# Experts of a mixture in blocks of 32 rows on four column groups of TensorE, with plain float32 weights

## The chip, the core and the metric

The kernel runs on one core of a Trainium2 chip. The metric is the time of one execution on the device in microseconds (us). An execution is also profiled; its trace gives the start, the duration and the releaser of each instruction and the packets of each DMA.

## What is computed

A trunk of two layers runs over 1280 tokens of width 1024 (256 of context, 1024 latent). Layer 0 mixes tokens by a convolution, layer 1 by gated linear attention, and each is followed by a hierarchical mixture of 32 experts: the best of 4 groups, then the best two of its 8 experts. Layer 0 routes 1280 tokens (2560 pairs of token and expert), layer 1 only the 1024 latent ones (2048 pairs). The expert itself is:

```python
def block_ffn(args):
    e, idx = args
    xb = h_pad[idx]
    return (jax.nn.silu(xb @ w1[e]) * (xb @ w3[e])) @ w2[e]
```

`w1[e]` and `w3[e]` are 1024 x 512, `w2[e]` is 512 x 1024, all float32: 6.29 MB an expert, 201 MB a layer. The sum over a token's two experts, weighted by the router, goes back into the residual. Everything is float32.

## The kernel before

Every phase is a function that writes one program for each engine, with semaphores between them and a barrier at its end: `front`, `conv_taps`, `conv_out`, then `route`, `experts` and `combine_values` for layer 0, then `gla_keys`, `gla_scan`, `gla_output`, and `route`, `experts`, `combine` for layer 1.

`route` sorts the pairs by expert into blocks of `BLK` = 128 rows, so that no block holds rows of two experts, and writes a plan: the token of each row, the expert of each block, and whether a block begins a new expert (`fresh`). The experts are taken in a fixed order, the first of each group, then the second of each, and so on.

`experts` runs over the blocks, whose number is known only at run time. For a block GpSimd gathers 128 token rows (L1335), TensorE turns them (`turn_x`, L1367), ScalarE and VectorE split the result into a high part in the short type fp32r and a low part, and the product with each weight is made of three fp32r matmuls of 512 columns (`product3`, L100 to L102). The weights are split in the same way, once an expert: ScalarE writes `moe_w_hi` (L1426), VectorE writes `moe_w_lo` (L1497). SyncE loads them ahead (L1295), each half of a matrix by a DMA of 1 MB: two buffers for `w1` and `w3`, one for `w2`; a load waits until VectorE has split what the buffer held. ScalarE takes the finished block out of PSUM (L1436) and stores it, a row of 1024 values to a row of `yd` (L1440). In the layer 0 pass SyncE also writes zeros into the blocks of `yd` that stay unused (L1320). `combine_values` and `combine` gather from `yd`.

`front` has the only matmuls of the kernel before that stand in column groups: `acc[j * STRIP:j * STRIP + 2, 0:P]` (L230), four outputs of 2 rows that begin at rows 0, 32, 64 and 96 of PSUM. It also loads tables of few rows from ScalarE's queue: `dw_w` has 31 rows, `pw1_b` 2, `norm_g` 8, and four tables one.

Of the kernel before, what the change touches and what calls it, by code (L numbers as in the profile page):

```python
# [27 lines left out]
GROUPS, PER_GROUP, EXPERTS, FF, BLK = 4, 8, 32, 512, 128  # L28
# [323 lines left out]
def conv_taps(nc, d, ht, vt, vecs, cs, mod, raw, ada_w, w2_raw):  # L352
# [3 lines left out]
    with ExitStack() as ctx:  # L356
# [12 lines left out]
        ahead = ph.sb("ahead", [P, CONV_W // 2 - 1])  # L369
        acc = [ph.sb(f"acc{q}", [P, HALF_OUT]) for q in range(2)]  # L370
# [21 lines left out]
        with nc.Block() as block:  # L392
# [39 lines left out]
            def _(pool):  # L432
                pool.memset(one[:, :], 1.0).then_inc(s("one_set"), 1)
                for b in range(2):
                    pool.memset(u[b][:, :, :], 0.0).then_inc(s("u_zero"), 1)
                for at in range(total):
# [49 lines left out]
            def _(act):  # L486
# [21 lines left out]
                for n in range(KC):  # L508
                    for g, (t0, m, c0) in enumerate(CONV_GROUPS):
# [13 lines left out]
                act.wait_ge(s("w2_hi"), KC)  # L523

# [462 lines left out]
def route(nc, d, layer, streams, plan, lg, ranks):  # L987

# [7 lines left out]
    with ExitStack() as ctx:  # L996
        ph = Phase(nc, ctx, f"route{layer}")
        s = ph.sem
        next_e = ph.sb("next_e", [P, EXPERTS])
        before = ph.sb("before", [P, P])  # L1000
        ones = ph.sb("ones", [P, P])
        ident = ph.sb("ident", [P, P])
        iota = ph.sb("iota", [P, P])
        token = ph.sb("token", [P, TILES])
        gm = ph.sb("gm", [P, nt])
        ga = ph.sb("ga", [P, nt, GROUPS])
        gsel = ph.sb("gsel", [P, nt, GROUPS])
        gw = ph.sb("gw", [P, nt])
        inner = [ph.sb(f"inner{j}", [P, nt, EXPERTS]) for j in range(2)]
        cand = ph.sb("cand", [P, nt, EXPERTS])  # L1010
        least = ph.sb("least", [P, nt])
        top = ph.sb("top", [P, 2, nt])
        hot = ph.sb("hot", [P, 2, nt, EXPERTS])
        both = ph.sb("both", [P, nt, EXPERTS])
        sofar = ph.sb("sofar", [P, nt + 1, EXPERTS])
        rank = ph.sb("rank", [P, nt, EXPERTS])
        picked = ph.sb("picked", [P, 2, nt, EXPERTS])
        mine = ph.sb("mine", [P, 2, nt])
        first = ph.sb("first", [P, 2, nt])
        over = ph.sb("over", [P, 2, nt])  # L1020
        steps = ph.sb("steps", [P, nt])
        more = ph.sb("more", [P, 2 * nt * nt + EXPERTS * nt])
        need = ph.sb("need", [P, EXPERTS])
        ends = [ph.sb(f"ends{j}", [P, EXPERTS]) for j in range(2)]
        passed = ph.sb("passed", [P, EXPERTS])
        blk_col = ph.sb("blk_col", [P, 1])
        blk = ph.sb("blk", [1, nb + 2])
        fresh = ph.sb("fresh", [1, nb])
        in_slot = ph.sb("in_slot", [P, 2 * nt, P])
        in_blk = ph.sb("in_blk", [P, 2 * nt, nb + 1])  # L1030
        pr = ph.ps("pr", [P, nt * EXPERTS])
        pa = ph.ps("pa", [P, nt * EXPERTS])
        pi = ph.ps("pi", [P, nb + 1])
        pb = ph.ps("pb", [1, P])

        with nc.Block() as block:
            @block.sync
            def _(sp):
                for dst, src in ((iota[:, :], d.iota), (before[:, :], d.before), (ones[:, :], d.ones), (token[:, :], d.token),
                                 (next_e[:, :], d.next_expert[0].partition_broadcast(P)), (ident[:, :], d.ident)):  # L1040
                    sp.dma_start(dst, src).then_inc(s("loaded"), 16)

            @block.tensor
            def _(pe):
                pe.wait_ge(s("loaded"), 96)
                pe.wait_ge(s("chosen"), 1)
                pe.matmul(pr[:, :], before[:, :], both[:, :, :].rearrange("p t e -> p (t e)"), start=True, stop=True)
# [21 lines left out]
            def _(dve):  # L1069
# [70 lines left out]
                for j in range(2):  # L1140
                    link(dve.tensor_tensor(picked[:, j, :, :], hot[:, j, :, :], rank[:, :, :], ALU.mult))
# [1997 lines left out]
```

## Time before, and how its profile is read

| what | us |
|---|---|
| median of 3 runs (lowest, highest) | 3011.33 (3010.84, 3011.63) |
| the profiled execution, and the span of its trace | 3014.36, 3012.5 |
| layer 0: route, from start to the start of experts | 688.9 to 726.5 |
| layer 0: experts, to the start of combine | 726.5 to 1526.0 |
| layer 1: route | 2277.2 to 2308.9 |
| layer 1: experts, to the start of combine | 2308.9 to 2933.0 |

PE is TensorE, PEld its loads of the stationary operand, DVE VectorE, ACT ScalarE, POOL GpSimd, SP SyncE; a queue of the DMA engines is named q0 (issued by GpSimd), q1 (by SyncE) or q10 (by ScalarE). A busy time is read against the stage in which it stands, and a mean over the span hides stages with different limits. Matmuls overlap, so their rate is read from the starts of groups. A plain float32 matmul leaves two records in the trace.

### The profile page before, as it was taken

The numbers are of one execution on the slowest core, as the hardware profiler recorded it, in microseconds if no ns is written. First come the engines' busy times: TensorE is split into PE (matmuls) and PEld (weight loads), VectorE is DVE, ScalarE is ACT, GpSimd is POOL, SyncE is SP. The second block draws the span as 40 slices with busy tenths as digits, with TensorE's granted clock in tenths as the row PEclk, the third lists the DMA queues.
The fourth block names the chain that finished last, engine by engine and source line by source line (L and its number), as shares of the span: only waits on it lengthen the run. The fifth ranks groups of instructions, "written<-read, shape, count | busy, mean of one in ns | idle before, by whom it ended". The sixth has DMA issues, their size and how long they took to land. (4 is left out here: it accounts for less than half of the span.)

```text
span 3012.5 us, 41138 instructions
## 1 busy us (share of the span) xinstructions
PE 2510.7 (83%) x13498; PEld 2036.1 (68%) x13498; DVE 1993.3 (66%) x2023; ACT 1449.3 (48%) x1624; POOL 346.5 (12%) x400
## 2 busy tenths in 40 slices
PE   6788761993999999999929989979694999999970
PEld 3567651883788888888818867768583788888850
DVE  3779998665767777688336203357665888888855
ACT  3210011551666666677234213367321777777742
POOL 1000001000001000011012110053100111111104
PEclk7789885995999999999969999989795999999985
DMA  7354332223798888899464321034553999999956
GB/s 273 126 169 141 127 140 73 87 98 108 296 340 317 320 312 298 321 389 388 159 217 171 119 64 28 8 114 169 208 179 101 382 389 387 390 386 390 398 212 224
DMA packets 292015, 679.43 MB, mean 226 GB/s; under 512 B 22974, under 2 KB 49934, under 8 KB 291912
## 3 DMA queue, kind: packets, MB, share of 16 engines
q1 hardware_dynamic: 261564, 575.75, 52.9%
q0 software_dynamic: 20064, 66.16, 6.5%
q10 hardware_dynamic: 10284, 36.16, 3.0%
q8 instruction: 64, 1.05, 0.1%
q14 instruction: 39, 0.31, 0.0%
HBM read 588.01 MB, written 90.00 MB: 225 GB/s over the span
## 5 line engine op out<-in xcount | busy, mean ns | idle before, releaser
L1497 DVE TENSOR_TENSOR moe_w_lo<-moe_w_raw,moe_w_hi 128x2048 fp32r<-128x2048 f32 x384 | 862.4, 2286 | 88.1 <-ACT moe_w_hi L1426 50.2
L1426 ACT ACTIVATE moe_w_hi<-moe_w_raw 128x2048 fp32r<-128x2048 f32 x384 | 714.3, 1909 | 66.9 <-issue 39.5
L100 PE MATMUL moe_pg<-moe_w_hi,moe_xt_hi 128*128 128x512 f32 x592 | 243.7, 412 | 11.5 <-DVE moe_xt_lo L1508 5.9
L100 PE MATMUL moe_py<-moe_w_hi,moe_at_hi 128*128 128x512 f32 x592 | 241.7, 408 | 11.9 <-DVE moe_w_lo L1497 8.2
L101 PE MATMUL moe_pg<-moe_w_lo,moe_xt_hi 128*128 128x512 f32 x592 | 237.2, 401 | 0.0
L102 PE MATMUL moe_pg<-moe_w_hi,moe_xt_lo 128*128 128x512 f32 x592 | 236.9, 400 | 0.0
L101 PE MATMUL moe_py<-moe_w_lo,moe_at_hi 128*128 128x512 f32 x592 | 235.0, 397 | 0.0
L102 PE MATMUL moe_py<-moe_w_hi,moe_at_lo 128*128 128x512 f32 x592 | 234.8, 397 | 0.0
L102 PE MATMUL moe_pu<-moe_w_hi,moe_xt_lo 128*128 128x512 f32 x592 | 234.3, 396 | 0.0
L100 PE MATMUL moe_pu<-moe_w_hi,moe_xt_hi 128*128 128x512 f32 x592 | 234.1, 396 | 0.0
L101 PE MATMUL moe_pu<-moe_w_lo,moe_xt_hi 128*128 128x512 f32 x592 | 234.1, 396 | 0.0
L1543 DVE TENSOR_TENSOR moe_a<-moe_sil,moe_pu 128x512 f32<-128x512 f32 x74 | 50.9, 688 | 176.2 <-issue 129.2
L1436 ACT ACTIVATE moe_y<-moe_py 128x1024 f32<-128x1024 f32 x74 | 76.0, 1026 | 147.6 <-PE moe_py L102 147.6
L513 ACT ACTIVATE taps_sg<-taps_zg,channel_vectors 128x512 f32<-128x512 f32 (+1 forms) x24 | 14.8, 615 | 269.2 <-PE taps_za L102 269.2
L1329 POOL COPY moe_idx<-plan_token 128x1 int32 (+1 forms) x76 | 16.0, 210 | 1074.7 <-PE moe_pxt L1367 1074.6
L1451 ACT ACTIVATE moe_xt_hi<-moe_pxt 128x1024 fp32r<-128x1024 f32 x74 | 75.8, 1024 | 132.1 <-PE moe_pxt L1367 132.1
L100 PEld LDWEIGHTS moe_pg<-moe_w_hi,moe_xt_hi 128*128 128x128 f32 x592 | 113.5, 192 | 36.7 <-issue 12.7
L100 PEld LDWEIGHTS moe_py<-moe_w_hi,moe_at_hi 128*128 128x128 f32 x592 | 112.0, 189 | 35.8 <-issue 12.3
L1335 POOL DMA_INDIRECT moe_xg<-scratch_experts_in,moe_idx x76 | 119.9, 1578 | 121.7 <-issue 121.7
L100 PE MATMUL taps_zg<-ht_conv_hi,taps_w_hi 128*128 128x512 f32 (+1 forms) x192 | 77.6, 404 | 65.5 <-DVE taps_w_lo L534 51.6
L102 PEld LDWEIGHTS moe_pg<-moe_w_hi,moe_xt_lo 128*128 128x128 f32 x592 | 113.3, 191 | 27.4
L102 PEld LDWEIGHTS moe_py<-moe_w_hi,moe_at_lo 128*128 128x128 f32 x592 | 112.0, 189 | 27.0
(367 smaller groups left out, 5445.0 us busy)
## 6 DMA issues: line engine op xcount, KB each, us to landing
moe_w_raw<-in_moe_w SPq DMA_DIRECT2D x384, 1024.0 KB, 12.8
taps_ada_w<-in_ada_w SPq DMA_DIRECT2D x40, 1024.0 KB, 7.0
scratch_experts_out<-moe_y ACTq DMA_DIRECT2D x57, 512.0 KB, 6.4
taps_raw<-in_conv_pw_w SPq DMA_DIRECT2D x20, 512.0 KB, 9.4
scan_v<-scratch_gla_values SPq DMA_DIRECT2D x20, 512.0 KB, 4.1
front_w<-in_ada_w SPq DMA_DIRECT2D x8, 1024.0 KB, 18.9
cv_raw<-in_gla_w_in SPq DMA_DIRECT2D x16, 512.0 KB, 3.9
scratch_gla_out<-scan_o SPq DMA_DIRECT2D x16, 512.0 KB, 6.6
```

Source lines behind the costliest of these rows:

```text
L100: pe.matmul(out, xh, wh, start=start, stop=False)
L101: pe.matmul(out, xh, wl, start=False, stop=False)
L102: return pe.matmul(out, xl, wh, start=False, stop=stop)
L513: act.activation(sg[g][:, 0:m], zg[g][:, 0:m], ACT.Sigmoid, bias=vecs[:, n, V_BG:V_BG + 1])\
L1329: pool.tensor_copy(idx[:, :], plan.token[:, ds(k, 1)]).then_inc(s("idx_ready"), 1)
L1335: pool.indirect_dma_start(xg[0:rows, :], None, d.hd[:, :], bass.IndirectOffsetOnAxis(idx[0:rows, :], 0))\
L1426: act.activation(hi[m][:, cut, :], raw[m][p][:, cut, :], ACT.Copy).then_inc(s(f"{m}_hi{h}"), 1)
L1436: act.activation(y[:, :], py[:, :], ACT.Copy).then_inc(s("y_out"), 1)
L1451: act.activation(xt_hi[:, :, :], pxt[:, :, :], ACT.Copy).then_inc(s("xt_hi"), 1)
L1497: dve.tensor_tensor(lo[m][:, cut, :], raw[m][p][:, cut, :], hi[m][:, cut, :].bitcast(F32), ALU.subtract).then_inc(s(f"{m}_lo{h}"), 1)
L1543: dve.tensor_tensor(a[:, :], sil[:, :], pu[:, :], ALU.mult).then_inc(s("a_ready"), 1)
```

## The change

Blocks have 32 rows. The weights are used as they are, in plain float32: nothing is split, and a product is one matmul with 32 stationary columns (rows of the block) and 256 moving columns of the weights. Four such matmuls write to the four column groups, the rows 0, 32, 64 and 96 of PSUM: a group j makes a quarter of the columns of the result. `a` and the block of results therefore stand with the quarter as the outer index of the partition, and the store writes them back as 4 quarters of 32 rows of 256 values. A block is gathered as 128 quarter rows.

`Feed` holds four whole buffers, each with all three matrices of an expert. SyncE loads the experts in the fixed order, the first three of them while `route` runs, the fourth when `experts` starts (`route` works in the fourth buffer), and expert x + 3 once the blocks of expert x - 1 are done. An expert without rows gets one block. `w1` and `w3` are loaded two rows together to a partition. TensorE's program is a loop over experts with a loop over the expert's blocks in it; the other engines loop over blocks, four to a turn. `route` computes no `fresh` flag and no expert of a block, but the last block of each expert (`plan.ends`), with 32-row slots. The zeros are written once for all blocks beyond the fewest, from ScalarE's queue in `conv_taps`; both layers' stores have one size.

```diff
-GROUPS, PER_GROUP, EXPERTS, FF, BLK = 4, 8, 32, 512, 128
+GROUPS, PER_GROUP, EXPERTS, FF, BLK = 4, 8, 32, 512, 32
+EXPERT_ORDER = [g * PER_GROUP + e for e in range(PER_GROUP) for g in range(GROUPS)]
+AHEAD_X = 4
...
+                        if g == 2 and n == 1:
+                            act.wait_ge(s("zeros_set"), 1)
+                            act.dma_start(d.yd[2 * TOK:, :].rearrange("(p r) (s n) -> p (r s) n", p=P, n=D // 4),
+                                          zeros[:, :].unsqueeze(1).to_broadcast([P, EXPERTS * BLK // P * 4, D // 4]))\
+                                .then_inc(s("covered"), 16)
...
+class Feed:
+    BUFS, AHEAD = 4, 3
+    PAIR = 2 * KC * FF
+    WORDS = PAIR + FF // P * D
...
+    def load_pair(self, sp, x):
+        e, b = EXPERT_ORDER[x], x % self.BUFS
+        for m, src in enumerate((self.d.w1, self.d.w3)):
+            for h in range(2):
+                sp.dma_start(self.pair[:, b, m, h * KC // 2:(h + 1) * KC // 2, :].rearrange("p (s c) n -> p s (c n)", c=2),
+                             src[self.layer, e, h * D // 2:(h + 1) * D // 2, :].rearrange("(s p c) n -> p s (c n)", p=P, c=2))\
+                    .then_inc(self.sem(f"pair_loaded{b}"), 16)
+    def load_back(self, sp, x):
+        e, b = EXPERT_ORDER[x], x % self.BUFS
+        for h in range(2):
+            sp.dma_start(self.back[:, b, 2 * h:2 * h + 2, :],
+                         self.d.w2[self.layer, e, h * FF // 2:(h + 1) * FF // 2, :].rearrange("(k p) n -> p k n", p=P))\
+                .then_inc(self.sem(f"back_loaded{b}"), 16)
...
+                for x in range(feed.AHEAD):
+                    feed.load_pair(sp, x)
+                    feed.load_back(sp, x)
...
-        SLOTS = {"w1": 2, "w3": 2, "w2": 1}
-        raw = {m: [ph.sb(f"{m}_raw{p}", sh) for p in range(SLOTS[m])] for m, sh in shapes.items()}
-        hi = {m: ph.sb(f"{m}_hi", sh, F32R) for m, sh in shapes.items()}
-        lo = {m: ph.sb(f"{m}_lo", sh, F32R) for m, sh in shapes.items()}
...
+        idx = ph.sb("idx", [P, UNROLL], I32)
+        xg = [ph.sb(f"xg{p}", [P, CUT]) for p in range(UNROLL)]
+        x_rows = ph.sb("x_rows", [P, CUT])
+        xt = ph.sb("xt", [P, 2, P])
+        sil = ph.sb("sil", [P, P])
+        a = ph.sb("a", [P, P])
+        at = ph.sb("at", [P, P])
+        y = [ph.sb(f"y{p}", [P, CUT]) for p in range(UNROLL)]
+        y_last = ph.sb("y_last", [P, CUT])
...
-                def bring(mats, k, least, p=0):
-                    def free(m, h):
-                        if SLOTS[m] == 1 and least:
-                            sp.wait_ge(s(f"{m}_lo{h}"), k)
-                        elif SLOTS[m] == 2 and least == 2:
-                            sp.wait_ge(s(f"{m}_lo{h}"), k - 1)
-                    def fresh():
-                        e = sp.value_load(plan.block[0:1, ds(k, 1)], min_val=0, max_val=EXPERTS - 1)
-                        for m in mats:
-                            for h in range(2):
-                                cut = slice(h * half[m], (h + 1) * half[m])
-                                free(m, h)
-                                sp.dma_start(raw[m][p][:, cut, :],
-                                             dram[m][layer, ds(e, 1), h * half[m] * P:(h + 1) * half[m] * P, :]
-                                             .rearrange("o (k p) n -> p (o k) n", p=P)).then_inc(s(f"{m}_raw{h}{p}"), 16)
...
+                for x in range(feed.AHEAD, BUFS):
+                    feed.load_pair(sp, x)
+                    feed.load_back(sp, x)
+                for x in range(EXPERTS):
+                    times = x // BUFS + 1
+                    sp.wait_ge(feed.sem(f"pair_loaded{x % BUFS}"), 64 * times)
+                    sp.sem_inc(s("pair_ready"), 1)
+                    sp.wait_ge(feed.sem(f"back_loaded{x % BUFS}"), 32 * times)
+                    sp.sem_inc(s("back_ready"), 1)
+                    if 1 <= x < EXPERTS - feed.AHEAD:
+                        done = sp.value_load(plan.ends[0:1, x - 1:x], min_val=1, max_val=nb)
+                        sp.wait_ge(s("pair_done"), done)
+                        feed.load_pair(sp, x + feed.AHEAD)
+                        sp.wait_ge(s("back_done"), done)
+                        feed.load_back(sp, x + feed.AHEAD)
...
+                    pool.indirect_dma_start(xg[p][:, :], None, cut_rows, bass.IndirectOffsetOnAxis(idx[:, p:p + 1], 0))\
+                        .then_inc(s(f"gathered{p}"), 16)
+                def body(k, i, p):
+                    pool.wait_ge(s("x_here"), k + 1)
+                    gather(k + UNROLL, p)
...
-                def out_product(n, before, least):
-                    pe.wait_ge(s("at_lo"), n)
-                    if least:
-                        pe.wait_ge(s("y_out"), before)
-                    for h in range(2):
-                        pe.wait_ge(s(f"w2_lo{h}"), n)
-                        for c in range(2):
-                            for k in range(h * half["w2"], (h + 1) * half["w2"]):
-                                cols = slice(c * N, (c + 1) * N)
-                                last = product3(pe, py[:, cols], at_hi[:, k, :], at_lo[:, k, :],
-                                                hi["w2"][:, k, cols], lo["w2"][:, k, cols], k == 0, k == FC - 1)
-                    last.then_inc(s("w2_done"), 1)
...
+                def out_product(out, buf):
+                    for c in range(STRIPS):
+                        for j in range(STRIPS):
+                            last = pe.matmul(out[j * BLK:(j + 1) * BLK, 0:CUT], at[:, c * BLK:(c + 1) * BLK],
+                                             feed.back[:, buf, c, j * CUT:(j + 1) * CUT], start=c == 0, stop=c == STRIPS - 1)
+                    last.then_inc(s("back_done"), 1)
+                def in_product(k, b):
+                    for c in range(KC):
+                        for j in range(STRIPS):
+                            last = pe.matmul(pg[j * BLK:(j + 1) * BLK, 0:2 * P].rearrange("t (m n) -> t m n", m=2),
+                                             xt[:, c % 2, (c // 2) * BLK:(c // 2 + 1) * BLK],
+                                             feed.pair[:, b, :, c, j * P:(j + 1) * P], start=c == 0, stop=c == KC - 1)
+                    last.then_inc(s("pair_done"), 1)
+                    turn_x(k + 1)
+                def before_out(k, experts_in, b):
+                    if started(k, 1):
+                        pe.wait_ge(s("at_ready"), k)
+                        pe.wait_ge(s("back_ready"), experts_in)
+                        pe.wait_ge(s("y_out"), k)
+                        out_product(py, b)
+                    pe.wait_ge(s("a_ready"), k + 1)
+                    pe.transpose(pat[:, 0:P], a[:, :], ident[:, :]).then_inc(s("at_turned"), 1)
+                def expert(x, b, first):
+                    pe.wait_ge(s("xt_ready"), first + 1)
+                    pe.wait_ge(s("pair_ready"), x + 1)
+                    in_product(first, b)
+                    end = pe.value_load(plan.ends[0:1, ds(x, 1)], min_val=1, max_val=nb)
+                    before_out(first, x, (b - 1) % BUFS)
+                    with pe.If(first + 1 < end):
+                        with pe.Fori(first + 1, end) as k:
+                            pe.wait_ge(s("xt_ready"), k + 1)
+                            in_product(k, b)
+                            before_out(k, x + 1, b)
+                    return end
...
+                def take_x(k):
+                    act.wait_ge(s("xt_turned"), k + 1)
+                    act.activation(xt[:, :, :], pxt[:, 0:2 * P].rearrange("p (c n) -> p c n", c=2), ACT.Copy)\
+                        .then_inc(s("xt_ready"), 1)
+                def store(k, src, stored):
+                    act.dma_start(d.yd[ds(k * BLK, BLK), :].rearrange("t (s n) -> s t n", n=CUT), src).then_inc(s(stored), 16)
+                def body(k, i, p):
+                    act.wait_ge(s("pair_done"), k + 1)
+                    if started(k, 1):
+                        act.wait_ge(s("a_ready"), k)
+                    act.activation(sil[:, :], pg[:, 0:P], ACT.Silu).then_inc(s("sil_ready"), 1)
+                    take_x(k + 1)
+                    if started(k, 1):
+                        b = (p - 1) % UNROLL
+                        act.wait_ge(s("back_done"), k)
+                        if started(k, UNROLL + 1):
+                            act.wait_ge(s(f"y_stored{b}"), (i - (1 if p == 0 else 0)) * 16)
+                        act.activation(y[b][:, :], py[:, 0:CUT], ACT.Copy).then_inc(s("y_out"), 1)
+                        act.wait_ge(s("y_out"), k + 1)
+                        store(k - 1, y[b][:, :], f"y_stored{b}")
...
-                def low(m, n, p=0, halves=(0, 1)):
-                    for h in halves:
-                        cut = slice(h * half[m], (h + 1) * half[m])
-                        dve.wait_ge(s(f"{m}_hi{h}"), n)
-                        dve.tensor_tensor(lo[m][:, cut, :], raw[m][p][:, cut, :], hi[m][:, cut, :].bitcast(F32),
-                                          ALU.subtract).then_inc(s(f"{m}_lo{h}"), 1)
...
+                def bring_x(k, i, p):
+                    dve.wait_ge(s(f"gathered{p}"), (i + 1) * 16)
+                    if started(k, 1):
+                        dve.wait_ge(s("xt_turned"), k)
+                    dve.tensor_copy(x_rows[:, :], xg[p][:, :]).then_inc(s("x_here"), 1)
+                def body(k, i, p):
+                    bring_x(k + 1, i + (p + 1) // UNROLL, (p + 1) % UNROLL)
+                    dve.wait_ge(s("sil_ready"), k + 1)
+                    if started(k, 1):
+                        dve.wait_ge(s("at_turned"), k)
+                    dve.tensor_tensor(a[:, :], sil[:, :], pg[:, P:2 * P], ALU.mult).then_inc(s("a_ready"), 1)
+                    dve.wait_ge(s("at_turned"), k + 1)
+                    dve.tensor_copy(at[:, :], pat[:, 0:P]).then_inc(s("at_ready"), 1)
```

TensorE, one block in the loop of layer 0. `moe_pxt` is the turned block, `moe_pu` and `moe_py` the products with `w3` and `w2`, `moe_pat` the turned activation. Before:

```order
L100 MATMUL moe_pu<-moe_w_hi,moe_xt_hi 128x512
L101 MATMUL moe_pu<-moe_w_lo,moe_xt_hi 128x512
L102 MATMUL moe_pu<-moe_w_hi,moe_xt_lo 128x512
L1367 MATMUL moe_pxt<-moe_ident,moe_xg 128x128 x8
L100 MATMUL moe_py<-moe_w_hi,moe_at_hi 128x512
L101 MATMUL moe_py<-moe_w_lo,moe_at_hi 128x512
L102 MATMUL moe_py<-moe_w_hi,moe_at_lo 128x512
...
L1406 MATMUL moe_pat<-moe_ident,moe_a 128x128 x4
```

And now, where `feed_w` is the four weight buffers:

```order
L1384 ISA
L1359 MATMUL moe_pg<-feed_w,moe_xt 32x256 x32
L1344 REGISTER_ALU
L1346 MATMUL moe_pxt<-moe_ident,moe_x_rows 128x128 x2
L1352 MATMUL moe_py<-feed_w,moe_at 32x256 x16
L1374 MATMUL moe_pat<-moe_ident,moe_a 128x128
L1384 REGISTER_ALU
L1384 COMPARE_AND_BRANCH
```

The 72 products of 512 columns and 12 transposes of a 128-row block became 48 products of 256 columns and 3 transposes of a 32-row block, in the same order of steps.

SyncE's loads in the loop of the kernel before, for `w1` and `w3` of one expert, with the look-up of whether and which:

```order
L1256 TENSOR_LOAD plan_fresh
L1256 ISA x2
L1257 COMPARE_AND_BRANCH
L1290 REGISTER_ALU
L1290 TENSOR_LOAD plan_block
L1290 ISA x2
L1287 REGISTER_ALU
L1295 ISA
L1295 DMA moe_w_raw<-in_moe_w 128x4x512
```

And now, for two experts that follow each other:

```order
L1310 TENSOR_LOAD plan_ends
L1310 ISA x2
L1023 DMA feed_w<-in_moe_w 128x2x1024 x4
L1030 DMA feed_w<-in_moe_w 128x2x1024 x2
L1310 TENSOR_LOAD plan_ends
```

The six loads of 1 MB an expert stayed; a row of a `w1` or `w3` load is now 1024 values, it was 512.

ScalarE's store in the loop before, and what stands around it:

```order
L1435 REGISTER_ALU
L1436 ACTIVATE moe_y<-moe_py 128x1024
L1440 ISA
L1440 DMA scratch_experts_out<-moe_y 128x1024
L1456 ACTIVATE moe_at_hi<-moe_pat 128x512
```

And now, a whole turn of the loop:

```order
L1422 ACTIVATE moe_sil<-moe_pg 128x128
L1410 REGISTER_ALU
L1411 ACTIVATE moe_xt<-moe_pxt 128x256
L1429 REGISTER_ALU
L1430 ACTIVATE moe_y<-moe_py 128x256
L1415 ISA
L1415 DMA scratch_experts_out<-moe_y 4x32x256
```

The store's destination went from 128 rows of 1024 to 4 times 32 rows of 256, and ScalarE has no weight work between the stores.

## Rows read from the trace of the kernel before

**Rows 1.** Windows by stage: us from:to, length, busy by engine, clock, DMA share, GB/s.
```profile
688.90:726.50 37.60, 11.84 (x46) 9.87 (x46) 27.73 (x86) 1.73 (x3) 0.00 (x0) 0.50 0.03 8
726.50:1526.00 799.50, 768.65 (x3536) 625.29 (x3536) 530.05 (x319) 488.07 (x361) 74.61 (x88) 0.98 0.84 306
825.00:1275.00 450.00, 450.00 (x2091) 366.77 (x2090) 307.09 (x186) 283.79 (x211) 43.17 (x50) 1.00 0.87 315
2277.20:2308.90 31.70, 9.69 (x38) 8.15 (x38) 24.25 (x84) 1.72 (x3) 0.00 (x0) 0.50 0.04 10
2308.90:2933.00 624.10, 587.64 (x2696) 477.72 (x2696) 506.35 (x289) 452.00 (x321) 64.95 (x68) 0.97 0.97 363
2400.00:2850.00 450.00, 450.00 (x2091) 366.75 (x2091) 393.47 (x224) 349.32 (x250) 45.55 (x50) 1.00 1.04 390
```
**Rows 2.** Costliest groups of the page: count, busy us, mean ns, idle before.
```profile
L1497 DVE TENSOR_TENSOR moe_w_lo<-moe_w_raw,moe_w_hi 128x2048 fp32r<-128x2048 f32 x384 | 862.4, 2286 | 88.1 <-ACT moe_w_hi L1426 50.2
```
**Rows 3.** The instructions that read or write `moe_y`: first and last start us.
```profile
L1436 ACT ACTIVATE moe_y<-moe_py x74: 1023/1026/1031, 781.4 to 2924.2; 128x1024 f32<-128x1024 f32 x74
```
**Rows 4.** Timeline of PE near 2033: start us, us, group, records.
```profile
2032.71 1.89 PE L2451 MATMUL scan_po<-scan_state,scan_qs 128*128 128x256 f32 x8
2034.44 1.89 PE L2460 MATMUL scan_pds<-scan_v,scan_kst 128*128 128x256 f32 x8
```
**Rows 5.** Timeline of PE in `front`, 71 to 76.
```profile
71.26 1.09 PE L213 MATMUL front_pt<-front_ident,front_xn 128*128 128x128 f32 x8 [0.28 <-ACT front_xn L287]
72.28 0.40 PE L226 MATMUL front_acc<-front_bias,front_one 1*2 1x128 f32 x8
72.61 1.93 PE L230 MATMUL front_acc<-front_w,silu_c 128*2 128x128 f32 x64
74.47 0.80 PE L236 MATMUL front_pp<-front_ident,front_ada_row 128*128 128x128 f32 x4
```
**Rows 6.** Groups of VectorE and of GpSimd, 2400 to 2850, by form.
```profile
L1543 DVE TENSOR_TENSOR moe_a<-moe_sil,moe_pu 128x512 f32<-128x512 f32 x25 | 17.2, 688 | 30.7 <-issue 30.7
...
L1335 POOL DMA_INDIRECT moe_xg<-scratch_experts_in,moe_idx x25 | 42.5, 1700 | 39.2 <-issue 39.2
```
**Rows 7.** DMA queues, 2400 to 2850: packets, MB, share of 16 engines.
```profile
q1 hardware_dynamic: 66242, 156.69, 92.7%
...
q10 hardware_dynamic: 2576, 8.91, 4.9%
```
**Rows 8.** The same, 43 to 48: q1 moves mostly rows of 512 bytes.
```profile
q1 hardware_dynamic: 1193, 0.90, 60.7%
```
**Rows 9.** DMA from 0 to 40: queue q10, and all that ACT issued.
```profile
q10 hardware_dynamic: 60, 0.16, 1.5%
...
front_rows<-in_conv_dw_w ACTq DMA_DIRECT2D x1, 124.0 KB
...
front_rows<-in_conv_dw_b ACTq DMA_DIRECT2D x1, 4.0 KB
front_rows<-in_conv_ln_g ACTq DMA_DIRECT2D x1, 4.0 KB
front_rows<-in_conv_ln_b ACTq DMA_DIRECT2D x1, 4.0 KB
front_rows<-in_conv_pw_b ACTq DMA_DIRECT2D x1, 8.0 KB
front_gain_row<-in_norm_g ACTq DMA_DIRECT2D x1, 4.0 KB
front_bias<-in_ada_b ACTq DMA_DIRECT2D x1, 8.0 KB
```
**Rows 10.** Timeline of SP's own queue, first 80 us: start, us, DMA, count.
```profile
4.46 32.39 SPq L169 DMA_DIRECT2D front_w<-in_ada_w  x8
```
**Rows 11.** The page: mean busy share of the DMA engines in 40 slices.
```profile
DMA  7354332223798888899464321034553999999956
```

More of the change, by code:

```diff
@@ L1021, in route @@
[L1021 to L1030, printed above, removed]
+        sb = feed.room()
@@ new lines, in route @@
+        before = sb([P, P])
+        ones = sb([P, P])
+        iota = sb([P, P])
+        token = sb([P, TILES])
+        strip = sb([P, 1])
+        gm = sb([P, nt])
+        ga = sb([P, nt, GROUPS])
+        gsel = sb([P, nt, GROUPS])
+        gw = sb([P, nt])
+        inner = [sb([P, nt, EXPERTS]) for j in range(2)]
+        cand = sb([P, nt, EXPERTS])
+        least = sb([P, nt])
+        top = sb([P, 2, nt])
+        hot = sb([P, 2, nt, EXPERTS])
+        both = sb([P, nt, EXPERTS])
+        sofar = sb([P, nt + 1, EXPERTS])
@@ L1056, in _ @@
                         pe.wait_ge(s("hot_slots"), 2 * (j // nt + 1))
-                    last = pe.matmul(pi[:, :], in_slot[:, j, :], in_blk[:, j, :], start=j == 0, stop=j == 2 * nt - 1)
+                    for r in range(0, P, BLK):
+                        last = pe.matmul(pi[r:r + BLK, :], in_slot[:, j, :], in_blk[:, j, :],
+                                         start=j == 0, stop=j == 2 * nt - 1)
                 last.then_inc(s("slots_done"), 1)
@@ L1361, in _, with turn_x @@
+                for k in range(UNROLL):
+                    gather(k, k)
+                blocks(pool, body, finish)
             @block.tensor
             def _(pe):
-                def turn_x(n):
-                    pe.wait_ge(s("gathered"), n * 16)
-                    for k in range(KC):
-                        last = pe.transpose(pxt[:, k, :], xg[:, k * P:(k + 1) * P], ident[:, :])
+                def turn_x(k):
+                    pe.wait_ge(s("x_here"), k + 1)
+                    for c in range(2):
+                        last = pe.transpose(pxt[:, c * P:(c + 1) * P], x_rows[:, c::2], ident[:, :])
@@ L1409, in _ @@
-                pe.wait_ge(s("ident"), 16)
-                turn_x(1)
-                blocks(pe, body, lambda count, last: out_product(count, last, 1))
+                def out_product(out, buf):
[4 more added lines that the diff above has]
+                    last.then_inc(s("back_done"), 1)
@@ new lines, in _ @@
+                pe.wait_ge(s("ident"), 16)
+                turn_x(0)
+                end = 0
+                for b in range(BUFS):
+                    end = expert(b, b, end)
+                with pe.Fori(1, EXPERTS // BUFS) as i:
+                    end = pe.value_load(plan.ends[0:1, ds(i * BUFS - 1, 1)], min_val=1, max_val=nb)
+                    for b in range(BUFS):
+                        end = expert(i * BUFS + b, b, end)
+                count = pe.value_load(plan.block[0:1, 0:1], min_val=plan.fewest, max_val=nb)
```

448 lines of the change are left out of this document (148 added, 300 removed).

## The prediction

> **What bounds the kernel now.** I read the windows by stage first, because a mean over the span would mix stages with different limits [rows 1]. In 825 to 1275 us (layer 0) and in 2400 to 2850 us (layer 1) PE is busy 450 of 450 us, so the experts stand on TensorE, and whatever DVE and ACT do there is beside it. The DMA share reads 0.87 and 1.04: in layer 1 the weights are nearly a second bound. From its route's start layer 0's mixture lasts 1526.0 − 688.9 = 837.1 us and layer 1's 2933.0 − 2277.2 = 655.8 us, 1492.9 together; I forecast these two and leave the rest as it is. The profiled execution took 3014.36 us, 3.0 above the median, so 3 comes off at the end.
>
> **How many blocks.** The routing follows from the inputs; I counted it by evaluating the reference. In blocks of 128 it gives 42 and 32, as the 74 copies to `moe_y` say [rows 3]. In blocks of 32, in the fixed order: layer 0 has 96, by expert 1, 2, 1, 12, 1, 1, 1, 8, 3, 1, 1, 6, 1, 2, 1, 8, 2, 1, 1, 11, 4, 1, 1, 2, 1, 1, 1, 3, 1, 1, 1, 14; layer 1 has 79, one to four an expert.
>
> **Cost of a block on TensorE.** A plain float32 matmul leaves two records. Eight of 256 columns take 2034.44 − 2032.71 = 1.73 us, 0.216 each, with all columns of the array in one matmul [rows 4]. The only column groups of the trace are in `front`: 64 records of 128 columns from 72.61 to 74.47 are 29 ns each, against 108 (half of 216) alone, so 3.7 go side by side; over a perfect four 1.86 − 1.73 = 0.13 us is left, which I read as the price of a change of shape [rows 5]. A new block has 32 + 16 matmuls, 96 records in 24 groups of four: 24 × 0.216 = 5.2 us. Three transposes at (72.28 − 71.26)/8 = 0.13 [rows 5] add 0.4, four changes of shape 0.5, and for short waits that no row shows I add 0.2: 6.3 us. These groups have 32 stationary columns where the row has 2. From below nothing beats 5.9, the sum with half the changes and no waits; from above, if the loads of the stationary operand do not hide (175 ns for 128 columns, 366.75/2091 [rows 1], so 44 ns for 32, 96 times 4.2 us, not far below 5.2), I take 7.5.
>
> **The other engines.** GpSimd needs 1.70 us for an indirect DMA and 39.2/25 = 1.57 of issue [rows 6], with the index copy some 3.5 us a block. DVE's product of 512 columns took 688 ns [rows 6]; three smaller ones are under 2.1. ACT has three copies no larger. All are under 6.3. Between a block's first products and its transpose stand ACT's silu and DVE's product, each under 0.69 us with its semaphore; out_product of the block before (8 × 0.216) and turn_x (0.26) cover that, 2.0 us; without cover it would be some 1 us a block. The splitting that goes (862.4 us of `moe_w_lo` alone [rows 2]) was hidden behind the busy PE and is worth nothing by itself. The zeros are 4.2 MB in `conv_taps`, where the DMA slices read 3 to 5 tenths [rows 11]: hidden; uncovered they are about 12 us.
>
> **Cost of an expert's loads.** q10's 25 stores moved 8.91 MB in 4 KB rows in 4.9% of 16 × 450 = 353 us of engine time, 40.5 ns a KB, or 25.2 GB/s an engine [rows 7]. The loads' rows are 4 KB now throughout, so an expert's 6.29 MB takes 15.6 us over 16 engines (404 GB/s together), 32 of them 499 us. Rows of 512 bytes cost more: 0.90 MB in 60.7% of 80 us is 55 ns a KB [rows 8]; for the 1 KB rows of gather and store I take 48, with bounds 40.5 and 55.
>
> **Cost of a store.** The store's outermost count goes from 128 to 4, and the trace shows what that does. Of the 60 packets of q10 in the first 40 us, 31 + 1 + 1 + 1 + 2 + 8 + 1 = 45 are rows of the seven tables; 15 are left [rows 9]. That is one for the 31-row table, 1 + 1 + 1 + 2 + 8 + 1 for the others: one for each engine used, where the number of engines divides the count of rows. The old stores fit too: 9 of 128 rows and 16 of 64 make 2176 packets, plus 16 each, 2576 [rows 7]. So a store whose outermost count is 4 goes to four engines, 32 KB each, besides 8 KB of the gather: 40 × 48 ns = 1.92 us a block on these four, bounds 1.62 and 2.2. A load is spread over all 16 and ends with the slowest, so this adds to the loads one for one. Spread over 16 it would be 16 × 48 ns = 0.77.
>
> The Trainium skill's page DMA: Bandwidth & Descriptors, section "Why a DMA increments its semaphore by 16 and not by 1", has the rule that k is the largest number up to 16 that divides the slowest dimensions of both sides, and that a hardware queue uses the lowest-numbered k engines. The trace's 60 packets agree with the first half; that it is always the same ones no run shows yet. By it the store has four engines, as in the sum; if the four changed from store to store, the sum would be that of the rival below.
>
> **The sum.** *Layer 0*, along what ends last: constants 2.5; loads of experts 0 to 3, 62.4 (three lie under route's 37.6, the fourth starts at 49, when its buffer is long free); 4 for the start of the products after the last one; 10 because SP signals a loaded expert only when it gets there, and it stands while its queue is full (8 issues took 32.39 us [rows 10], some 4 each, two or three of them ahead of the signal); expert 3's 12 blocks, 75.6, in which the loads run out of free buffers; then 25 loads, 390, with the stores of 66 blocks, 126.7; expert 31's 14 blocks, 88.2; 10 from the last copy to the end, 2924.2 to 2933.0 in the old [rows 1, 3]. That is 769.4, or 67.7 less. In the next long one, expert 19's 11 blocks (69 us), three loads (47) and 11 stores (21) fit, so the loads do not stop again and nothing more is added. *Layer 1*: 2.5 + 499.2 + 75 × 1.92 + 4 × 6.3 + 10 = 680.9, or 25.1 more: PE is no longer the bound, the four engines are. Together −42.6: 3014.4 − 42.6 − 3 = 2969 us at the median.
>
> SP's six issues an expert stay behind a wait for `pair_done` of the expert two before; behind that wait are the signals of the next expert, hence the 10, once, at the first long expert. In later ones the loads are the chain, so a late signal costs only where PE then ends last. PE's granted clock reads 0.50 (1.2 GHz) in route, where PE is busy 11.84 of 37.60 us [rows 1]; a single-block expert at that level takes 12.6, still under its load of 17.5, so I add nothing; on the long runs it could be some 9.
>
> **The rivals.**
>
> *The store is harmless.* Its rows spread over the engines, or the four overlap the loads of others. Then 0.77 takes the place of 1.92: 141 × 1.15 = 162 less, and 24 given back (a walk through the counts) because the loads, now ahead, stand while the long experts, above all expert 19, hold the buffers. 2969 − 138 = 2831 us. For it: the loads have 16 engines and a queue of their own. Against it: the 15 packets.
>
> *Slower: column groups of 32 overlap less.* At 7.5 us a block, TensorE ends last in layer 0: 35.6 for the rest of route, 11 for the first products, 96 × 7.5 = 720, 50 of waits before single-block experts (a walk through the counts, loads at 15.6, stores at 1.92), 10 at the end: 827. Layer 1 stays with the loads, 680.9 + 4 × 1.2 = 686. The sum is 1513, 20 above before: 3032 us. It decides from about 7.1 us, where the same walk gives 1493. For it: the nearest row has 2 stationary columns, the loads of 32 have no row, and 64 of them a product go with groups that are refilled each 54 ns. Against it: 3.7 of 4 [rows 5].
>
> The Trainium skill's page TensorE: Matmul & The Clock Gate, Part 3, on packing small matmuls in column tiles, measured 2.38 times for three tiles of 32 columns, 0.79 of the ideal. By that the 5.2 would be 6.6 and the block 7.5 to 7.7, this rival. The trace's 3.7 of 4 speaks against it, at other sizes.
>
> *The groups do not overlap at all.* 96 × 0.216 = 20.7, a block 22 us, 96 + 79 of them 3850: some 2400 above before. The 3.7 of 4 [rows 5] excludes it but for the width.
>
> **How the numbers follow.** A measurement of this kernel tells about 0.2% (6 us) from no change. Forecast case 0.56: its own range is 2915 to 3010 (1.62 or 2.2 for 141 blocks is −42 or +39; the block at 5.9 or 6.9 is −12 or +25; SP's 10 may be 0 or 25). Of it 0.47 is faster, 0.05 same, 0.04 slower. Harmless store 0.18, all faster. Lesser overlap 0.22, and none 0.04, all slower: 0.26. Faster 0.65, same 0.05, slower 0.30. The range runs from just under the harmless store, 2815, to just above the lesser overlap, 3045, and leaves out the last case and the tails.
>
> **What the profile would show.** Right: in layer 1 PE is busy well under the window, idle before L1359 and released by SP; DMA lists q10's packets of 1 KB with four completion packets a store; some engines' share is near 1 and the mean share clearly below; a 12- or 14-block expert has starts of blocks 6.3 us apart; layer 0 near 770, layer 1 near 680. Wrong: 16 completion packets a store, or layer 1 under 620 (the store is harmless); blocks 7.1 us or more apart with PE busy (overlap); a store or a gather waited for by ACT or DVE in each block, which none of the cases has; or SP's signals tens of us behind their loads at many experts.

## The result and the profile after

The changed kernel takes 2995.97 us (median of five runs, 2992.86 to 2997.88) against 3010.91 beside it: a ratio of 0.9947, 95% interval 0.9934 to 0.9959. The direction was forecast and the time lies in the range, but 15 us came where 42 were forecast. The profiled execution has a span of 2994.9 us, against 3012.5.

The windows of the changed kernel, in the columns of [rows 1]: layer 0's mixture from the start of its route, then its stretch after the first long expert; layer 1's, then its 450 us in the middle:

```profile
688.40:1486.30 797.90, 631.32 (x9670) 341.26 (x9670) 108.30 (x367) 103.62 (x293) 115.94 (x200) 0.89 0.73 285
851.00:1380.00 529.00, 432.51 (x6542) 230.26 (x6539) 57.89 (x199) 69.06 (x199) 76.42 (x132) 0.90 0.84 329
2239.40:2915.50 676.10, 523.38 (x7955) 281.04 (x7955) 90.53 (x314) 85.86 (x242) 96.21 (x166) 0.89 0.89 330
2400.00:2850.00 450.00, 374.10 (x5643) 199.22 (x5639) 49.86 (x171) 59.51 (x171) 65.60 (x114) 0.92 0.96 351
```

Layer 0 went from 837.1 to 797.9 (−39.2; forecast −67.7), layer 1 from 655.8 to 676.1 (+20.3; forecast +25.1). TensorE is no longer busy throughout, and the DMA engines aren't either in layer 0: 0.84 in a stretch that should have been one chain of loads. The timeline of PE inside expert 3's twelve blocks (start, us, group, records):

```profile
801.42 0.33 PE L1374 MATMUL moe_pat<-moe_ident,moe_a 128*128 128x128 f32 x1
801.68 3.66 PE L1359 MATMUL moe_pg<-feed_w,moe_xt 128*32 128x256 f32 x64
805.27 0.50 PE L1346 MATMUL moe_pxt<-moe_ident,moe_x_rows 128*128 128x128 f32 x2
805.70 1.93 PE L1352 MATMUL moe_py<-feed_w,moe_at 128*32 128x256 f32 x32
807.57 0.33 PE L1374 MATMUL moe_pat<-moe_ident,moe_a 128*128 128x128 f32 x1
807.82 3.66 PE L1359 MATMUL moe_pg<-feed_w,moe_xt 128*32 128x256 f32 x64
```

From first product to first product (L1359) a block takes 807.82 − 801.68 = 6.14 us; 6.3 was forecast. The block on TensorE is not where the gain went. What TensorE waits for in layer 0 (waiter, releaser: us, times, longest):

```profile
PE moe_pg L1359 <- SPq L1305: 95.2, 16, 13.0
PE moe_pxt L1346 <- SPq L1305: 22.6, 1, 22.6
```

Line 1305 is SP's `sem_inc(s("pair_ready"), 1)`, so TensorE waits for SP to say that an expert is loaded. Whether the load itself was late is a separate question. SP waited for a load in layer 0 only twice, both times at expert 31, when every load had been issued:

```profile
SPq L1305 <- DMA feed_w<-in_moe_w: 10.3, 1, 10.3
SPq L1307 <- DMA feed_w<-in_moe_w: 5.9, 1, 5.9
```

SP's own timeline around experts 7 to 10, with the loads of `w1` and `w3` (L1023) and of `w2` (L1030):

```profile
848.43 2.06 SPq L1023 DMA_DIRECT2D feed_w<-in_moe_w  x4
856.87 0.88 SPq L1030 DMA_DIRECT2D feed_w<-in_moe_w  x2
858.52 3.88 SPq L1023 DMA_DIRECT2D feed_w<-in_moe_w  x4
868.16 0.88 SPq L1030 DMA_DIRECT2D feed_w<-in_moe_w  x2
869.80 11.23 SPq L1023 DMA_DIRECT2D feed_w<-in_moe_w  x4
881.07 5.43 SPq L1030 DMA_DIRECT2D feed_w<-in_moe_w  x2
887.26 9.92 SPq L1023 DMA_DIRECT2D feed_w<-in_moe_w  x4
```

The first two rows load expert 7, the next two expert 8, then 9. Adding up the packets of q1, expert 7 had landed at 866.9 us. SP was then waiting to issue expert 8's `w2` (for the last product of the expert that held the buffer), and next it stood 11.23 and 5.43 us in expert 9's loads, which took 2.06 and 0.88 us where the queue was empty; it reached the signal at 886.5, and expert 7's first product began at 886.7, 20 us after the weights were there. The same sum for other experts, in us from the route's start, beside the first experiment below:

```
layer expert blocks | changed: landed, first product, later by | e1_direct: the same
0      3     12     |  67.9    87.0   19.1 |  67.9   83.9   16.0
0      7      8     | 178.5   198.2   19.8 | 176.8   191.2  14.4
0     15      8     | 343.9   366.3   22.4 | 332.2   337.3   5.1
0     19     11     | 433.6   455.0   21.5 | 416.3   421.3   5.0
0     25      1     | 581.7   604.8   23.1 | 548.5   548.4  -0.1
0     31     14     | 692.6   691.3   -1.2 | 660.4   655.2  -5.2
1     15      3     | 288.9   319.0   30.1 | 294.6   301.5   6.8
1     31      4     | 615.7   632.7   17.0 | 623.3   617.3  -6.0
```

(A negative number: the first product needs `w1` and `w3` only, and `w2` landed last. Lateness includes the time in which TensorE was still busy with the experts before; in the changed kernel TensorE waited for SP's signal in all rows but the two of expert 31 and that of layer 1's expert 15, whose signal came 0.7 us before its first product.) The loads then stop in layer 0. DMA by 40 slices of 9 us, 850 to 1210 us of the changed kernel:

```profile
DMA  9999999324999999938999999631799999962111
GB/s 401 409 411 408 410 408 413 153 78 134 414 325 418 411 415 410 413 143 306 415 412 414 413 410 411 243 123 36 287 413 414 412 414 410 413 243 111 42 45 38
```

The dips at slices 8 to 10, 18, 26 to 29 and 36 to 40 are the long experts 7, 11, 15 and 19: each began 20 us late, so it held its buffer 20 us longer than needed, and the three loads ahead were done before it was. From the packets, expert 3's own stop (its blocks are in the forecast) is 35.6 us; those after it are 13.7 us behind expert 7, 13.3 behind 15, 31.7 behind 19 and 4.9 behind the four blocks of 20, 63.6 in all.

### The profile page after: what moved, and what is told of

Its sections match the earlier page's. It is cut to its first block and busy times, and to the rows that moved or that the text cites. A ratio compares the mean times of both kernels' runs of the same rounds, so it can differ in the third digit from the quotient of the medians.

```text
span 2994.9 us, 61160 instructions
## 1 busy us (share of the span) xinstructions
PE 2291.2 (77%) x24807; PEld 1541.1 (51%) x24808; DVE 1103.5 (37%) x1927; ACT 695.4 (23%) x1470; POOL 420.1 (14%) x610
## 5 line engine op out<-in xcount | busy, mean ns | idle before, releaser
L1359 PE MATMUL moe_pg<-feed_w,moe_xt 128*32 128x256 f32 x11200 | 700.2, 406 | 189.8 <-SPq L1305 182.1
L1359 PEld LDWEIGHTS moe_pg<-feed_w,moe_xt 128*32 128x32 f32 x11200 | 366.8, 117 | 463.3 <-SPq L1305 185.5
L1352 PE MATMUL moe_py<-feed_w,moe_at 128*32 128x256 f32 x5536 | 334.6, 382 | 0.0
L1352 PEld LDWEIGHTS moe_py<-feed_w,moe_at 128*32 128x32 f32 x5536 | 161.8, 110 | 110.4
L103 PE MATMUL cv_acc<-cv_w_hi,ht_next_hi 128*128 128x512 f32 x288 | 116.9, 406 | 15.5 <-DVE ht_next_lo L1972 15.5
L105 PE MATMUL cv_acc<-cv_w_hi,ht_next_lo 128*128 128x512 f32 x288 | 116.3, 404 | 0.0
L104 PE MATMUL cv_acc<-cv_w_lo,ht_next_hi 128*128 128x512 f32 x288 | 115.5, 401 | 0.0
L579 DVE SCALAR_TENSOR_TENSOR taps_acc<-taps_back,channel_vectors,taps_acc 128x649 f32<-128x649 f32 x120 | 107.0, 892 | 0.0
L567 DVE SCALAR_TENSOR_TENSOR taps_acc<-taps_u,taps_both,taps_acc 128x649 f32<-128x649 f32 x120 | 107.0, 891 | 0.0
L594 DVE SCALAR_TENSOR_TENSOR taps_acc<-taps_ahead,channel_vectors,taps_acc 128x649 f32<-128x649 f32 x112 | 91.9, 888 | 0.0
## 6 DMA issues: line engine op xcount, KB each, us to landing
front_w<-in_ada_w SPq DMA_DIRECT2D x8, 1024.0 KB, 18.9
```

The lines of the kernel that those rows point to most:

```text
L103: pe.matmul(out, xh, wh, start=start, stop=False)
L104: pe.matmul(out, xh, wl, start=False, stop=False)
L105: return pe.matmul(out, xl, wh, start=False, stop=stop)
L567: dve.scalar_tensor_tensor(acc[0][:, :], src, tap, acc[0][:, :], ALU.mult, ALU.add)\
L579: dve.scalar_tensor_tensor(acc[1][:, :], src, tap, acc[1][:, :], ALU.mult, ALU.add)\
L594: dve.scalar_tensor_tensor(acc[q][:, :], src, tap, acc[q][:, :], ALU.mult, ALU.add)\
```

## The experiments

Each compares with the kernel before on the same chip, where that took 3010.91 to 3012.1 us; stage times are of the profiled executions, layer 0 and layer 1 from the route's start. The changed kernel has 797.9 and 676.1.

**e1_direct.** TensorE waits for the loads' own semaphores, so SP waits for no load:

```diff
-                    sp.wait_ge(feed.sem(f"pair_loaded{x % BUFS}"), 64 * times)
-                    sp.sem_inc(s("pair_ready"), 1)
...
-                    pe.wait_ge(s("pair_ready"), x + 1)
+                    pe.wait_ge(feed.sem(f"pair_loaded{b}"), (i + 1) * 64)
```

(and the same for `back_loaded`, 32 a turn.)

> TensorE waits for the loads' own semaphores; SP no longer waits for a load and signals nothing. Theory L (late signals): in the changed kernel's trace the first product of an expert starts 17 to 36 us after its load has landed, because SP stands while it issues the next loads; in layer 0 that opens stops of the loads at the long experts. Then expert 3 should start near 758 instead of 775 us, the loads of experts 7 to 31 should run nearly without stops (25 x 15.3 + 66 x 1.8 = 502 us instead of 529), and layer 0's mixture should be 40 us shorter (798 to 758), layer 1's some 14 (676 to 662): about 2940 us. Rival H (the long experts hold the buffers whatever is signalled): only the 17 us at expert 3 and the end are gained, the four stops stay: 2970 to 2990 us.

2945.23 us, ratio 0.9775 (0.9758 to 0.9791), 51 us less than the changed kernel. Layer 0 is 764.6, layer 1 660.7: −33 and −15, where 40 and 14 were expected. Expert 3's start, expected some 17 us earlier, moved by 3 (87.0 to 83.9): its signal was not what held it, see e8_ident. The table above shows the lateness of the first products down to some 5 us from expert 15 on, and the stops after expert 3's are 11.3 us in all, 63.6 in the changed kernel; expert 19's alone is 1.0 for 31.7, as the forecast had it ("the loads do not stop again"). Of the 52 us less of stops only some 30 came back: from the end of expert 3's stop to the last landing, stops left out, the loads took 490 us (468 in the changed kernel), with 66 and 67 stores in that time. That fits stores which had run while the loads stood and now lie beside loads. Theory L holds; rival H (2970 to 2990) falls. TensorE's waits in layer 0 are now:

```profile
PE moe_pg L1353 <- DMA feed_w<-in_moe_w: 60.1, 8, 11.5
PE moe_pxt L1340 <- DMA moe_ident<-const_ident: 22.5, 1, 22.5
```

**e2_store16.** The store in four pieces, one a column group, the signals as in the changed kernel:

```diff
-                    act.dma_start(d.yd[ds(k * BLK, BLK), :].rearrange("t (s n) -> s t n", n=CUT), src).then_inc(s(stored), 16)
+                    for j in range(STRIPS):
+                        act.dma_start(d.yd[ds(k * BLK, BLK), j * CUT:(j + 1) * CUT], src[j * BLK:(j + 1) * BLK, :])\
+                            .then_inc(s(stored), 16)
```

> The store of a block is made of four stores of 32 rows of 256 values, one for each column group; everything else is as in the changed kernel. Theory F (the store with 4 as its outermost count uses four engines and adds some 1.8 us to the loads for each block): 32 rows use 16 engines, a block adds some 0.75, layer 1's mixture falls from 676 to about 600 us, layer 0's by 30 to 60: about 2880 us. The completion packets of q10 become 64 a block, they were 4. Rival G (the loads are slowed by something else, gather or memory): within 10 us of the changed kernel, about 2996.

2899.08 us, ratio 0.9624 (0.9608 to 0.9641): layer 0 768.2, layer 1 612.9. Queue q10 in layer 1's mixture, first of the changed kernel, with 79 stores of 128 rows:

```profile
q10 hardware_dynamic: 10428, 10.36, 4.4%
```

and of e2_store16:

```profile
q10 hardware_dynamic: 15168, 10.37, 5.4%
```

Of the first, 316 packets are small, 4 a block; of the second 5056, 64 a block: one for each engine that a store uses, as read from [rows 9], so four engines and 4 x 16. The bytes are the same and layer 1 is 63 us shorter, so the cost was where the bytes lay. Theory F holds, and rival G (no change) falls; 600 was expected for layer 1, so its size was a little too large.

**e3_both.** Both edits.

> Both edits: TensorE waits for the loads themselves, and the store is made of four stores of 32 rows. Theories L and F together: layer 0 near 720 us, then bound by TensorE in its long experts, layer 1 near 595: about 2835 us. If the late signals are no cost once the store is cheap, or the other way round, it is that of the better of the two alone.

2853.36 us, ratio 0.947 (0.9454 to 0.9485); run again beside e8_ident, 2853.44. Layer 0 736.3, layer 1 596.3. The two gains, 51 and 97, add up nearly (143); 2835 was expected, with 720 for layer 0. The loads, now ahead, stand 23.7 us for expert 19's eleven blocks and 44 in all behind expert 3; the prediction's rival of a harmless store gave back 24 for such stops.

> The kernel of e3_both once more, beside e8_ident on the same chip, as its measure: 2853 us within 4.

**e4_turns.** Only the order of the loops over column group and contraction, in both products:

```diff
-                    for c in range(KC):
-                        for j in range(STRIPS):
+                    for j in range(STRIPS):
+                        for c in range(KC):
                             last = pe.matmul(pg[j * BLK:(j + 1) * BLK, 0:2 * P].rearrange("t (m n) -> t m n", m=2),
```

> The products of a column group follow one another (group outside, contraction inside), instead of the four groups in turn; all else as in the changed kernel. Theory O (6.15 us a block come from four column groups side by side): with neighbours in one group 96 records of 0.216 and the rest give some 22 us a block, 175 blocks some 3850 us against 1474 for both mixtures now: about 5400 us. Rival (the order doesn't matter, records of 32 columns are simply cheaper): 6.15 us a block and 2996 us.

4590.8 us, a single run. A block of it on PE:

```profile
3707.98 0.33 PE L1374 MATMUL moe_pat<-moe_ident,moe_a 128*128 128x128 f32 x1
3708.24 11.50 PE L1359 MATMUL moe_pg<-feed_w,moe_xt 128*32 128x256 f32 x64
3719.67 0.50 PE L1346 MATMUL moe_pxt<-moe_ident,moe_x_rows 128*128 128x128 f32 x2
3720.10 4.59 PE L1352 MATMUL moe_py<-feed_w,moe_at 128*32 128x256 f32 x32
3724.63 0.33 PE L1374 MATMUL moe_pat<-moe_ident,moe_a 128*128 128x128 f32 x1
```

The same 96 records take 16.65 us a block, not 6.14. So the order makes the overlap: theory O holds in kind. It expected 22 us a block. In the trace neighbours of one group start 0.216 us apart, but where one group ends and the next begins a few records of both run side by side, which I had not counted.

**e5_store2.** As e1_direct, with the store in two pieces of two column groups:

```diff
+                    for j in (0, 2):
+                        act.dma_start(d.yd[ds(k * BLK, BLK), j * CUT:(j + 2) * CUT].rearrange("t (s n) -> s t n", n=CUT),
+                                      src[j * BLK:(j + 2) * BLK, :]).then_inc(s(stored), 16)
```

> As e1_direct, but a block's store is made of two stores, each with 2 as its outermost count (two column groups each). Theory F2 (such a store uses two engines, and always the same two): these two carry 64 KB of store and 8 of gather for each block instead of 32 and 8, at 40.5 ns a KB 1.3 us more; 75 blocks of layer 1 add 97 us to e1_direct's 661, layer 0 some 60 to 85: about 3110 us, with 4 completion packets a block as before. Rival S (the engines change from one store to the next, so that the load is the same as with one store on four): e1_direct's 2945 us within 10.

3188.41 us, ratio 1.0592 (1.0575 to 1.061): 243 us over e1_direct. Layer 1 768.9 (+108, 97 expected), layer 0 897.4 (+133, 60 to 85 expected). The 316 small packets of q10 in layer 1 are 2 for each of 158 stores. Rival S, engines that change from store to store, falls: the same bytes in two halves would have cost nothing. It is dearer than expected. ACT now stands in its own issues, as SP does in the changed kernel, its silu comes late, and TensorE waits for ACT through `moe_a` (ACT in the middle of layer 1; then layer 1's waits):

```profile
2600.70 10.99 ACTq L1410 DMA_DIRECT2D scratch_experts_out<-moe_y  x2
2612.00 0.28 ACT L1418 ACTIVATE moe_sil<-moe_pg 128x128 f32<-128x128 f32 x1 [11.46 <-issue]
ACT moe_sil L1418 <- issue: 328.5, 31, 16.7
PE moe_pat L1368 <- DVE moe_a L1454: 145.6, 31, 11.7
```

ACT spends 420 us of layer 1 in the issues of its 158 stores, where e1_direct has 45 us for 79 and e3_both 106 for 316. How much of the 243 us comes by this way and how much by the loads alone, no run separates. The second issue a block isn't the cost by itself: e3_both has four and is 92 us faster than e1_direct.

**e6_late_loads.** As e1_direct, with the first three experts loaded when `experts` starts:

```diff
-                for x in range(feed.AHEAD):
-                    feed.load_pair(sp, x)
-                    feed.load_back(sp, x)
...
-                for x in range(feed.AHEAD, BUFS):
+                for x in range(BUFS):
```

> As e1_direct, but the first three experts are loaded when the experts' phase starts, not while the routing runs. Theory P (the loads are the chain from the first one on): layer 1's mixture grows by about the routing's 31 to 33 us, 661 to 693; in layer 0, where the first products start 55 us after the routing's start whatever is loaded, expert 3 starts some 15 to 20 us later: about 2993 us. Rival (the loads have slack and catch up): within 10 us of 2945.

2983.35 us, ratio 0.9916 (0.99 to 0.9933), some 40 over e1_direct: layer 1 689.9 (+29), layer 0 776.2 (+12). Theory P holds: the loads are the chain of layer 1 from the first one on. That prefetch alone is worth more than twice what the whole change gained.

**e7_rows2k.** As e3_both, `w1` and `w3` with rows of 2 KB:

```diff
-                             src[self.layer, e, h * D // 2:(h + 1) * D // 2, :].rearrange("(s p c) n -> p s (c n)", p=P, c=2))\
+                             src[self.layer, e, h * D // 2:(h + 1) * D // 2, :].rearrange("(k p) n -> p k n", p=P))\
...
-                        last = pe.transpose(pxt[:, c * P:(c + 1) * P], x_rows[:, c::2], ident[:, :])
+                        last = pe.transpose(pxt[:, c * P:(c + 1) * P], x_rows[:, c * P:(c + 1) * P], ident[:, :])
```

> As e3_both, but w1 and w3 are loaded with rows of 512 values (2 KB), as the kernel before did, instead of two rows together (4 KB). Theory R (shorter rows cost the loads time: 45 ns a KB, between 40.5 for 4 KB and 55 for 512 bytes): 4.2 MB of an expert's 6.3 take 1.2 us longer, layer 1 grows from 596 to about 630, layer 0 by some 20: about 2905 us. Rival (2 KB rows move as fast): 2853 us within 6.

2873.75 us, ratio 0.9543 (0.9527 to 0.9559): 20 us over e3_both where 52 were expected, 15 of them in layer 1 (611.2), where 34 were. Row length counts, at less than half the price that I had interpolated.

**e8_ident.** As e3_both, with one line moved from SP to ACT: `dma_start(ident[:, :], d.ident)`. It is the 64 KB identity. In the changed kernel the first transposes waited for it; the second row of PE's waits above puts those 22.6 us down to SP's signal, which came in the same microsecond, and the same row of e1_direct to the identity, as does the row of PE's own weight load in the changed kernel:

```profile
PEld moe_pxt L1346 <- DMA moe_ident<-const_ident: 22.8, 1, 22.8
```

> As e3_both, but the 64 KB identity for the transposes is loaded from ACT's queue, not from SP's behind the loads of three experts. In the changed kernel's trace it takes 17.4 us to land and the first transposes wait for it until 742.4 us, when their rows have been there since 732.5. Theory I (this wait sets expert 3's start in layer 0): layer 0 is 8 to 10 us shorter, layer 1, where the loads are the chain, the same: about 2844 us. Rival (the identity still lands late, or the loads of the first experts set the start): 2853 us within 4.

2842.51 us, ratio 0.9436 (0.9423 to 0.9449), 11 below e3_both beside it. The identity lands in 5.8 us, and layer 0's expert 3 starts 74.0 us from the route's start instead of 83.8; layer 1 is 594.1 against 596.0. Theory I holds. Layer 0 is 721.9 against 737.6 in the profiled executions, 15.7 less where 8 to 10 were expected: behind the earlier start the stop at expert 7 is 5 us shorter too (8.6 for 13.7), which no run explains. This is the fastest version: 5.6% below the kernel before.

## Why the prediction was wrong

Where the forecast's sum and the trace part, in us from the route's start:

| | forecast | measured |
|---|---|---|
| layer 0: expert 3's first product | 79 | 87.0 |
| expert 31's first product | 671 | 691.3 |
| end | 769.4 | 797.9 |
| layer 1: the last load has landed | 646 | 615.7 |
| expert 31's first product | 646 | 632.7 |
| end | 680.9 | 676.1 |

- **The step that failed** is SP's late signal: "10 because SP signals a loaded expert only when it gets there", "hence the 10, once", and "a late signal costs only where PE then ends last". The mechanism was named and mis-sized. It isn't one delay: SP's signal came 12 to 34 us after the expert's last byte at 55 of the 64 experts, 40 to 68 us at seven in layer 0, where SP stood for a buffer as well, and before it only at the last of each layer. At expert 3, where the forecast put its one 10, taking the signal out gave 3. I assumed that behind it a chain of loads absorbs the rest. In layer 0 it doesn't, as a late long expert also frees its buffer late, and then the loads themselves stand. The prediction's signs of being wrong named it ("SP's signals tens of us behind their loads at many experts"), without a price. e1_direct measures it: 33 us in layer 0, 15 at the end of layer 1, 49 together where 10 stood in the sum. With it out, layer 0 takes 764.6 us, near the forecast 769.4, with the errors below against each other.
- **The store on four engines** was right in kind, by packets and by e2, e3 and e5, and too dear at 1.92 us a block. The loads of experts 13 to 28 of layer 1 take 309 us in the changed kernel, with some 37 stores among their packets, and 271 in e3_both, with some 39. At 15.6 us an expert (the second of layer 1 landed 15.4 after the first) that leaves 1.6 and 0.6 a block for 1.92 and 0.77, so four engines cost 1.0 more than 16; 1.15 was forecast. The first lies at my lower bound of 1.62. Which part of it, gather or store, is cheaper, no run separates. Only some 70 stores, not 75, were among layer 1's loads when the last one landed. Together this put the last landing 30 us too late in layer 1's sum and hid the other error: layer 1 came out within 5 us for two wrong reasons.
- **The start of layer 0** is 8 us later than forecast. I let it end with expert 3's load and the signal; the identity behind the loads, which stands in no term of the sum, held the first products back, and without that expert 3 starts 10 us earlier (e8_ident).
- **The end** of each layer is 8 us longer: in layer 0 from the last copy out of PSUM to the next phase 13.6 us (1472.75 to 1486.3) where I had taken 10 from the old 8.8, and from expert 31's first product to that copy 93.1 where 88.2 stood for its 14 blocks. No run asked why.
- **The block on TensorE**, 6.3 forecast, 6.14 measured, and the rival of lesser overlap (7.5) is out. That rival's page of the Trainium skill, TensorE: Matmul & The Clock Gate, Part 3, with its measured 2.38 for three tiles of 32 columns (0.79 of the ideal), does not describe this case: four records start within 0.02 us of each other, every 0.216 us, the full four.
- **The harmless store** (2831) was no description of the changed kernel, but it is close to what e3_both gives (2853), where the late signals are out as well.
- **Hidden or zero**: the zeros, as the time outside the mixtures changed by 1.3 us (span −17.6, mixtures −18.9), and GpSimd's gathers, for which VectorE waited once in layer 0 (11.6 us, at the first block). That the splitting was hidden rests on PE's 450 of 450 us [rows 1]; no run tested it.

The Trainium skill's rule on the engines of a DMA (DMA: Bandwidth & Descriptors, "Why a DMA increments its semaphore by 16 and not by 1") has a second half that e5_store2 bears out in part: engines that change from store to store would have left it at e1_direct's time, and it took 243 us more. That they are the lowest-numbered ones no run here shows.

## What to carry to other kernels

When one engine both issues loads and announces them, price the announcement at every item, not at the fill: it comes after everything that the engine issues first, and with a full queue six issues took 17 us here instead of 3, and signals came 12 to 34 us late; let the consumer wait for the load's own semaphore. A store's outermost count decided on how many DMA engines it lay, and beside the stream of loads the bytes on the fullest engine counted: a store of 128 KB cost some 1.6 us on four engines and 0.6 on 16, and halving the four cost 243 us with all that waits behind it, more than ten times what the whole change gained. A sum that agrees stage by stage only at its end may hold two errors, so compare it at the points between.

## What the runs showed that I had not expected

- A load of 64 KB issued behind weights that were still on their way took 16.9 us to land, and 5.8 us from another engine's queue (e8_ident).
- After a wait the first block of an expert is slow. The first of layer 0 came after TensorE had idled 22.57 us; beside it a block in the middle of expert 3 (columns of [rows 1]; the same 64 records of products, and in the second row the two transposes behind them):

```profile
743.60:749.60 6.00, 6.00 (x64) 2.73 (x64) 0.00 (x0) 0.00 (x0) 1.16 (x2) 0.58 1.02 407
801.68:805.27 3.59, 3.59 (x66) 1.98 (x65) 0.59 (x2) 0.34 (x1) 1.16 (x2) 1.00 0.93 373
```

The granted clock is 0.58 in the one (mostly the level of 1.2 GHz) and 1.00 (2.4 GHz) in the other. In layer 0 the first blocks of the experts with several took 7.6 to 9.1 us where TensorE had idled 2.9 to 13 us before them, and 6.15 where it had idled less than 1 us. The granted clock of those slow ones is 0.67 to 0.80, of experts 8, 16 and 31, at 6.15 us, 1.00. Expert 1's is the exception: 9.03 us without such a wait, at a granted clock of 1.00, so something else held it.
